# The last MLP units and the first units of the next projection taken by token tile, and the S5 products on tiles of the TensorE array

## The reference

```python
# end of the first block
h = rmsnorm(x, norm_mlp_g[l])
x = x + jnp.square(jax.nn.relu(h @ w_up[l])) @ w_down[l]      # 2048 -> 8192 -> 2048
return rmsnorm(x, norm_final_g)
...
# start of the second block
h = _rms(x, norm_g[l, 0]) * (1.0 + scale_m) + shift_m
proj = (h @ w_in[l]).astype(f32)                               # da_q, da_k, da_v, ..., s5_u
...
# S5 branch: 32 groups of 16 channels with 64 states each
bu = jnp.einsum('sgc,gpc->sgp', us, bb)                        # real and imaginary part
... (associative scan over tokens) ...
y = jnp.einsum('sgp,gcp->sgc', xr, c_re) - jnp.einsum('sgp,gcp->sgc', xi, c_im) + d_skip * us
```

## Time and profile before

| | |
|---|---|
| median of 3 runs | 2720.89 us (2720.29, 2720.89, and one of 9454.43) |
| the profiled execution | 2721.06 us, its span 2719.3 us |
| PE busy | 2650.8 us, 97% |
| DVE, ACT, POOL busy | 1906.8, 1254.7, 281.9 us |
| granted TensorE clock, mean | 0.992 |

### The profile page before, as it was taken

How to read it: one execution, slowest core, us unless ns; L and a number is a source line. 1 busy time by engine, 2 the same in 40 slices (tenths; PEclk the granted TensorE clock), 3 DMA queues, 4 the chain that set the end, 5 groups by cost and what they waited for, 6 DMA issues and landing times.

```text
span 2719.3 us, 36265 instructions
## 1 busy us (share of the span) xinstructions
PE 2650.8 (97%) x13230; PEld 2237.7 (82%) x13230; DVE 1906.8 (70%) x2275; ACT 1254.7 (46%) x1519; POOL 281.9 (10%) x322
## 2 busy tenths in 40 slices
PE   8999999999999998999999999999999999999997
PEld 8998888888888887898977788777778888888886
DVE  6777677788778777665686778687755555555687
ACT  5445544444444445455555444444554444444443
POOL 0040041324132000071000000000000000000000
PEclk9999999999999998999999999999999999999999
DMA  9646687788778885756554655588656656666784
GB/s 343 215 163 214 219 278 257 266 276 273 263 264 276 270 271 165 228 171 208 164 169 151 223 200 174 189 300 284 217 178 193 188 191 192 187 191 191 257 291 165
DMA packets 294705, 606.18 MB, mean 223 GB/s; under 512 B 25873, under 2 KB 26065, under 8 KB 292673
## 3 DMA queue, kind: packets, MB, share of 16 engines
q1 hardware_dynamic: 290272, 578.55, 64.8%
q0 software_dynamic: 4320, 26.13, 2.6%
HBM read 593.31 MB, written 11.29 MB: 222 GB/s over the span
## 4 chain that ended last, share of the span: by engine, by line
PE 86%; DVE 6%; ACT 3%; DMA 2%; issue 2%; POOL 0%; SPq 0%; DVEq 0%; ACTq 0%; POOLq 0%
PE ps L540 84%; DVE w_lo L1780 2%; ACT w_hi L1178 1%; DMA w_raw<-in_w_in 1%; DVE arena L1775 1%; PE ps L645 1%; DMA w_raw<-in_w_up 1%; DMA w_raw<-in_w_gate 0%; ACT arena L1209 0%; DVE x L1790 0%; PE ps L672 0%; PE ps L635 0%; DMA arena<-gain_scratch 0%; PE ps L656 0%; DVE arena L2375 0%
## 5 line engine op out<-in xcount | busy, mean ns | idle before, releaser
L1780 DVE TENSOR_TENSOR w_lo<-w_raw,w_hi 128x1024 fp32r<-128x1024 f32 x904 | 1127.0, 1250 | 765.0 <-ACT w_hi L1178 757.2
L1178 ACT ACTIVATE w_hi<-w_raw 128x1024 fp32r<-128x1024 f32 x904 | 951.1, 1054 | 1375.8 <-PE ps L540 1283.0
L540 PE MATMUL ps<-w_hi,hop_hi_part 128*128 128x512 f32 x2144 | 846.7, 395 | 8.1 <-issue 2.5
L540 PE MATMUL ps<-w_hi,hop_lo_part 128*128 128x512 f32 x2144 | 836.9, 390 | 0.0
L540 PE MATMUL ps<-w_lo,hop_hi_part 128*128 128x512 f32 x2144 | 836.8, 390 | 0.0
L540 PEld LDWEIGHTS ps<-w_hi,hop_hi_part 128*128 128x128 f32 x2144 | 403.9, 188 | 100.8 <-issue 13.4
L540 PEld LDWEIGHTS ps<-w_hi,hop_lo_part 128*128 128x128 f32 x2144 | 403.7, 188 | 85.1
L540 PEld LDWEIGHTS ps<-w_lo,hop_hi_part 128*128 128x128 f32 x2144 | 404.1, 188 | 81.6
L540 PE MATMUL ps<-w_hi,hid_hi_part 128*128 128x512 f32 x992 | 389.1, 392 | 2.8 <-DVE hid_lo_part L2447 1.5
L540 PE MATMUL ps<-w_hi,hid_lo_part 128*128 128x512 f32 x992 | 386.3, 389 | 0.0
L540 PE MATMUL ps<-w_lo,hid_hi_part 128*128 128x512 f32 x992 | 386.0, 389 | 0.0
(11 more groups left out here) (302 smaller groups left out, 1462.8 us busy)
## 6 DMA issues: line engine op xcount, KB each, us to landing
arena<-in_ada_w SPq DMA_DIRECT2D x256, 384.0 KB, 4.7
w_raw<-in_ffn_w_in SPq DMA_DIRECT2D x176, 512.0 KB, 3.5
w_raw<-in_w_in SPq DMA_DIRECT2D x152, 512.0 KB, 3.6
w_raw<-in_w_up SPq DMA_DIRECT2D x128, 512.0 KB, 3.9
w_raw<-in_w_down SPq DMA_DIRECT2D x128, 512.0 KB, 4.7
w_raw<-in_w_gate SPq DMA_DIRECT2D x128, 512.0 KB, 4.0
w_raw<-in_ffn_w_out SPq DMA_DIRECT2D x88, 512.0 KB, 3.6
w_raw<-in_w_out SPq DMA_DIRECT2D x64, 512.0 KB, 5.1
```

Of the source, the lines that this page charges most:

```text
L540: return nc.tensor.matmul(o, w, r, start=start, stop=stop, skip_group_check=True)
L1178: return nc.scalar.activation(o, i, ACT.Copy, scale=scale)
L1780: V.tensor_tensor(w_lo[:, j % LEAD, :, 0:cols], w_raw[:, j % RAW, :, 0:cols], w_hi[:, j % LEAD, :, 0:cols].bitcast(F32), ALU.subtract).the ...
```

## The change

1. The last four MLP units (20 to 23) run for token tile 0 first (four `token_half`), then for tile 1. DVE and ACT add, multiply and square the two parts per tile (`last_part`, `half_square`), and the variance and inverse root are made per tile.
2. The transposes of tile 0 (`turn_half(5, 0, ...)`) stand in front of the last `token_half` of the MLP. The first four projection units run for tile 0, then for tile 1, in the way of the FFN seam (`staggered_chunk`, shared by both now). For this the first chunk is da_v with `token_unit`, and the third is da_k with `unit`.
3. The ada slices of the last stretch stand at loop steps 0 to 15 (before 0 to 18), and PE's `modulation` after unit 17 (before 21).
4. `s5_input` takes the upper or lower 64 rows alone, in the order 0, 2, 1, 3; `s5_product` holds 32 columns and writes 32 partitions of bank 6.

```diff
-ADA_TAIL = [k + k // 4 for k in range(KT)]
+ADA_TAIL = list(range(KT))
...
         def last_group(u):
-            if u == 21:
+            if u == 17:
                 modulation((G_MLP + MLP_SUPER // 2) * KT)
-        down(R, 16, H + 3, 0, 1, MLP_SUPER, between=last_group)
...
+        for n in range(2):
+            token_chunk(R, 16 + UB * n, H + 3, n, hid_hi[:, 1], hid_lo[:, 1], UB, between=last_group)
+        for n in range(2):
+            pe.wait_ge(drained[n], H + 5)
         pe.wait_ge(sem["mod_ready"], G_IN2)
-        turn_scaled(5, 0)
+        for t in range(TT):
+            for q in range(STAGGER):
+                n, k = 2 + q // UB, q % UB
+                if t == 0:
+                    pe.wait_ge(sem["lo_ready"], R * 8 + (20 + q + 1))
+                elif q == 3:
+                    turn_half(5, 0, SCALED_TOK)
+                m = token_half(20 + q, n % 2, t, hid_hi[:, 1], hid_lo[:, 1], UK * k, k == 0, k == UB - 1)
+                if t == 1:
+                    m.then_inc(sem["unit_done"], 1)
+                elif k == UB - 1:
+                    m.then_inc(sem["half_done"], 1)
...
+        staggered_chunk(5, R_IN2, H_IN2, SCALED_TOK)
+        for c in range(1, 4):
+            chunk(R_IN2, UA * c, H_IN2 + c // 2, c % 2, ftiles=1 if c == 3 else FT, between=gain_steps)
...
-            for ii in range(4):
-                m = mm(PS[4 + ii // 2][:, (ii % 2) * S:(ii % 2 + 1) * S], span(S5_B[t % 2] + 2 * part, ii * P, P),
-                       T(40 + t), start=ii % 2 == 0)
+            for ii in (0, 2, 1, 3):
+                rows = slice(64 * (ii // 2), 64 * (ii // 2) + 64)
+                m = mm(PS[4 + ii // 2][:, (ii % 2) * S:(ii % 2 + 1) * S], span(S5_B[t % 2] + 2 * part, ii * P, P)[rows],
+                       T(40 + t)[rows], start=ii % 2 == 0)
...
-                m = mm(PS[6][:, 0:S], span(S5_C[t % 2] + 2 * part, ii * P, P), ROT[part][:, ii],
-                       start=part == 0 and ii == 0, stop=part == 1 and ii == 3)
+                own = 2 * S5_CH * ii
+                m = mm(PS[6][own:own + 2 * S5_CH, 0:S], span(S5_C[t % 2] + 2 * part, ii * P + own, 2 * S5_CH), ROT[part][:, ii],
+                       start=part == 0, stop=part == 1)
```

On ACT, behind the MLP loop (`both_squares(0)` stands at its step 18):

```diff
+        both_squares(1)
+        half_square(2, 0, 4)
+        half_square(3, 0, 8).then_inc(sem["tok_sums"], 1)
+        pair_guess(3, 0)
+        split(R_IN2, 0)
+        half_square(2, 1, 24)
+        split(R_IN2, 1)
+        hi_half(5, 0, 0)
+        hi_half(5, 0, 1)
+        half_square(3, 1, 28).then_inc(sem["tok_sums"], 1)
+        hi_half(5, 0, 2)
+        hi_half(5, 0, 3)
+        pair_guess(4, 1)
+        split(R_IN2, 2)
+        split(R_IN2, 3)
```

On DVE, behind the MLP loop (the modulation stands at its step 18, the addition of part 1 at step 19):

```diff
+        last_part(2, 0)
+        last_part(3, 0)
+        pair_variance(3, 0)
+        last_part(2, 1)
+        pair_inverse(3, 0)
+        mid_scaled(0, half(0)).then_inc(sem["rows_ready"], 1)
+        split(R_IN2, 0)
+        for b in range(2):
+            turned_half(5, 0, b, gain5, 0)
+        lo_half(5, 0, 0)
+        last_part(3, 1)
+        split(R_IN2, 1)
+        lo_half(5, 0, 1)
+        for b in range(2, STAGGER):
+            turned_half(5, 0, b, gain5, 0)
+        pair_variance(4, 1)
+        lo_half(5, 0, 2)
+        lo_half(5, 0, 3)
+        split(R_IN2, 2)
+        pair_inverse(4, 1)
+        mid_scaled(1, half(0)).then_inc(sem["rows_ready"], 1)
+        split(R_IN2, 3)
```

More of the change, by code:

```diff
@@ L848, in gain_steps @@
                 pe.wait_ge(sem["gain_ready"], 1)
-                pe.wait_ge(sem["xT_ready"], TURNED[5] + 4)
+                pe.wait_ge(sem["xT_ready"], TURNED[5] + 10)
                 turn_gain(4)
[L852 to L857, removed]
+        staggered_chunk(5, R_IN2, H_IN2, SCALED_TOK)
+        for c in range(1, 4):
+            chunk(R_IN2, UA * c, H_IN2 + c // 2, c % 2, ftiles=1 if c == 3 else FT, between=gain_steps)
         modulation((G_IN2 + 1) * KT, 6)
@@ L1449, in _ @@
                 projection_unit(c, q)
[L1451 to L1452 removed]
+                if c == 0 and q == 0:
+                    rest_rows(5, 3, gain5, 0)
                 if (c, q) == (1, 6):
@@ L1834, in lo_pair @@
                             ALU.subtract).then_inc(sem["hop_ready"], 2)
-        def scale_rows(dst, src, i):
-            for c in range(4):
-                for t in range(TT):
-                    m = V.tensor_scalar(dst[:, t, part(c)], src[:, t, part(c)], inverse(i, t), None, ALU.mult)
-                m.then_inc(sem["rows_ready"], 1)
         def of_arena(t):
@@ L2134, in _, with last_part @@
-        then(V.tensor_scalar(mid, mid, 1.0 / D, EPS, ALU.mult, ALU.add))
-        stt(both, mid, EPS, both, ALU.mult, ALU.add).then_inc(sem["tok_var"], 1)
-        token_inverse(3, SUM_MID, 2)
-        scale_rows(SCALED_TOK, Y_TOK, SUM_Y)
-        for b in range(4):
-            lo_pair(5, b)
+                    m = gained(t, n)
+                m.then_inc(sem["mid_gained"], 1)
+        def last_part(n, t):
+            k = 2 * t + n - 2
+            if t == 0:
+                dve.wait_ge(sem["half_done"], n - 1)
+            else:
+                dve.wait_ge(sem["unit_done"], (R_MLP + 29) * 8 + 20 + UB * (n - 1))
+            V.tensor_tensor(x_tok[:, t, part(n)], SETS[n % 2][t][:], x_tok[:, t, part(n)], ALU.add).then_inc(sem["mid_added"], 1)
+            dve.wait_ge(sem["mid_added"], k + 1)
+            gained(t, n).then_inc(sem["mid_gained"], 1)
+            if t == 1:
+                dve.sem_inc(drained[n % 2], 1)
@@ new lines, in pair_variance @@
+        def pair_variance(k, t):
+            mid, both = (tok_var[:, TT * i + t:TT * i + t + 1] for i in (SUM_MID, SUM_Y))
+            dve.wait_ge(sem["tok_sums"], k)
+            V.reduce_sum(mid, sums[:, SUM_MID, t], axis=AX_X)
+            then(V.reduce_sum(both, sums[:, SUM_Y, t], axis=AX_X))
+            V.tensor_scalar(both, both, 1.0 / D, None, ALU.mult)
+            then(V.tensor_scalar(mid, mid, 1.0 / D, EPS, ALU.mult, ALU.add))
+            stt(both, mid, EPS, both, ALU.mult, ALU.add).then_inc(sem["tok_var"], 1)
@@ new lines, in pair_inverse, with mid_scaled @@
+        def pair_inverse(k, t):
+            cols = slice(TT * SUM_MID + t, TT * SUM_Y + t + 1, TT)
+            dve.wait_ge(sem["tok_guess"], k)
+            then(newton(tok_inv[:, cols], tok_var[:, cols], tok_guess[:, cols]))
+        def mid_scaled(t, cols):
+            return V.tensor_scalar(SCALED_TOK[:, t, cols], Y_TOK[:, t, cols], inverse(SUM_Y, t), None, ALU.mult)
+        last_part(2, 0)
[3 more added lines that the diff above has]
+        pair_inverse(3, 0)
@@ L2142, in projection_unit @@
+        split(R_IN2, 3)
+        mid_scaled(0, part(2))
+        mid_scaled(1, part(2)).then_inc(sem["rows_ready"], 1)
+        turned_half(5, 1, 0, gain5, 0)
+        turned_half(5, 1, 1, gain5, 0)
+        for b in range(STAGGER):
+            lo_half(5, 1, b)
+            if b < 2:
+                turned_half(5, 1, b + 2, gain5, 0)
+        mid_scaled(0, part(3))
+        mid_scaled(1, part(3)).then_inc(sem["rows_ready"], 1)
         def projection_unit(c, q):
```

255 lines of the change are left out of this document (122 added, 133 removed).

## The result

| | before | changed |
|---|---|---|
| median | 2722.67 us (5 runs) | 2705.86 us (5 runs) |
| runs | 2720.29 to 2723.72 and the one of 9454.43 | 2704.38 to 2709.75 |
| the profiled execution, its span | 2721.06 us, 2719.3 us | 2709.75 us, 2708.0 us |

The ratio of the times is 0.9943, with a 95% interval of 0.9929 to 0.9956: 15.5 us less (12 to 19), clear of no change though far under 2%. The forecast was 2709 us, 12 us less, in a range of 2703 to 2719. The one run of 9454.43 us is not explained; the ratio leaves it out.

The account below looks back on a forecast made before the run. PE was taken as the bound, busy 2650.8 of 2719.3 us. S5 11.0 us (3.4 + 7.0 + 0.6) and the seam 1.0 make 12 us off the profiled 2721.06: 2709 us, range 2703 to 2719.

Parts of the forecast that it names:

- The seam gives more: Rival on the passage from MLP to projection: no falls of the clock, quicker DVE, 5 us gained, 2705 us; 13%.
- All four side by side: S5 products: the four 32-column matmuls run together, 0.86 us a group, 0.87 less, 7.0 us for eight groups.
- half side by side: Rival on S5 products: matmuls start only in order, 1.5 us a group, 0.23 less, time 2714 us; 17%.
- one behind the other: Rival on S5 products: the four column tiles run serially, 2.15 us a group, time 2719 us; 10%.
- every tile pays: Slower rival on S5 products: each column tile pays for getting in and out, 3.4 us a group, 2730 us; 4%.
- the price of getting in and out: S5 groups on small tiles: a cost on top of streaming, 0.41 to 0.43 us, read from groups on 64-row halves.
- S5 inputs: Input groups on 64-row halves: 1.31 us instead of 1.73, 0.42 less each, 3.4 us for eight.
- What standing together and starting from an idle PE add: S5: three adjacent product and input groups pay once, five products start from idle; up to 1.6 us, 0.6 taken.
- The waits for L2405 stay: S5 products: PE's four waits for DVE, 5.4 us, remain because PE's units start DVE's steps there.
- ACT splits it only behind the guess: First projection chunk: reason given for 3.0 us idle at unit 2, the guess needing tile 1's variance.
- restarts 0.6: Seam: the term for PE restarts, 0.6 us, within 56.2 us of work, restarts and idle time.
- The clock in the seam: Two falls to 0.50 cost 2.4 us, leaving 1.0 us gain; over 7 us at 0.5 would show the prediction wrong.

Follow-up runs that it names:

- e4: The changed kernel with all four S5 products of a group on one column tile (the S5 output is then wrong): 2717.19 us.
- e1: The changed kernel with both S5 steps as before, so the new seam alone: 2720.86 us, ratio 0.9987 to the kernel before.
- e2: The kernel before with only the two S5 steps put on tiles, seam as before: 2708.47 us, ratio 0.9946 to the kernel before.
- e8: The changed kernel with ACT instead of DVE moving the third and fourth part of the turned tile 0 out of PSUM: 2703.99 us.
- e11: The changed kernel run again as it is: 2706.16 us, ratio 0.9932 to the kernel before.
- e7: The changed kernel with PE waiting for each accumulation set separately and ACT moving two turned parts of tile 0 for DVE: 2704.88 us.
- e6: The changed kernel with ACT rounding projection unit 2 earlier, ahead of the third part of the activations and the guess for tile 1: 2703.08 us.
- e3: The changed kernel with the S5 inputs issued in the order 0, 1, 2, 3 instead of 0, 2, 1, 3: 2706.67 us.
- e5: The changed kernel with PE waiting for each accumulation set separately, and for the modulation only ahead of tile 0's transposes: 2703.11 us.

## Why the prediction was right, and where it was off

The forecast of 2709 us was 3 us too high, and its sign, its order of causes (S5 far ahead of the seam) and the idle times' places were right. The median of 2705.86 us lies beside the 2705 of "The seam gives more", but that rival is not what happened: of the missing 3 us the traces show 1.8 in the S5 groups, and the rest can't be put down to one place. The interval of 0.9929 to 0.9956 also shows that a change well under the 54 us that the prediction named can be told from none.

- **S5 products on four column tiles.** "All four side by side" held (group cost, starts within 0.02 us, and e4), and with it fell the three rivals on them: half side by side (1.5 us a group), one behind the other (2.15) and every tile pays (3.4). A group measured 0.77 us for 0.86. The mis-sized term is the price of getting in and out: 0.765 - 0.432 = 0.33 us here, not the 0.43 of the 64-row halves; for the 64-row inputs it is 0.40. Eight times 0.97 us are 7.7 for 7.0.
- **S5 inputs.** 1.27 us for 1.31: 0.46 less each, 3.7 us for 3.4.
- **What standing together and starting from an idle PE add.** I took 0.6; the traces give 12.8 - 7.7 - 3.7 = 1.4 us. About 0.9 of it come from the five products behind a wait: alone, a full group costs 1.97 us there for 1.73, a tiled one 0.84 for 0.77. The rest is the three places where both stand together: 1.90 us, where a product behind a wait and an input group would make 0.84 + 1.27 = 2.11. So "pay once for getting in and out" was too much: 0.2 us are saved, not the whole price.
- **The rest of the S5 stretch.** A further 2.4 us in this pair of traces were not in the sum: 0.7 us of wait and 1.7 us of low clock at the first product. They are not the change's: e1 and e2 show the wait and the fall going either way, by when the gate weights land. Without them the stretch gives 12.8 us, and the forecast's 11.0 is short by 1.8.
- **"The waits for L2405 stay."** Right: 4.7 us for 5.4, in four.
- **The seam.** Idle times forecast 0.5, 2.4, 1.9, 0.5, 1.4, 3.0, 1.0, 0.1, 1.2, 0.7, 0.6; measured 0.43, 2.13, 1.46, 0.35, 1.17, 2.57, 0.41, none, 1.35, 0.48, 0.27. Each stands where it was put; the sum is 10.6 for 13.3. Of the 1.9 for 1.46 us a part is a slip of the sum: the terms written down for tile 0 end at 13.55, not 13.8. For the 2.57 us the reason given ("ACT splits it only behind the guess") holds for 0.63 us; e8 shows DVE's row as the larger part.
- **The work in the seam.** The piece that the prediction puts at 56.2 us at full clock took 55.9 us in e11, which had no fall there. But idle time was 10.7 us of it, so work and restarts were 45.2 us for 42.9. The mis-sized term is "restarts 0.6": it should have been 2.9. In part this is how the rows count, since an idle time begins at a matmul's modelled end, 0.39 us behind its start, and a matmul costs only a step of 0.227; ten idle times hide 1.6 us so. The two errors cancel, and that the length came out right is luck.
- **The clock in the seam.** Two falls of 3.4 us for 2.4 us was right for the profiled run: 107.70 against 105.1 us without a fall, 2.6 us, so the seam gives 1.1 us in the pair of profiles for 1.0 forecast. It was not right for the kernel: of six traces with the changed seam two had no fall, one a single fall of 6.8 us, and two had 10.2 us at 0.50, which cost 4.2 us and is beyond the 7 us that the prediction named as a sign of being wrong. Over all traces the stretch takes 107.4 against 108.0 us, with a spread of 4 us, so "about 1 us" is the best that can be said; in a run without a fall it is 2.9.
- **The end of the program.** The sum had no term for it. The kernels with the new seam take 2 us more there on average, which is of the size of what the seam gives; that the seam is the cause is not shown beyond the split into two and eleven traces.
- **The run itself.** The sum was made on one profiled execution. The start to unit 17 differs by up to 5.6 us between runs of nearly the same code, which is as large as most terms of this prediction. That the profiled time met the forecast to 0.8 us is luck: 3.6 us more at the start and 2.9 at the end stand against 4.3 more in the S5 stretch and 1.5 between seam and S5, none of which was in the sum.

Still open: what decides whether the clock falls behind the same idle time, why the start varies, and why the write near the end lands later with the new seam.

## To carry to other kernels

Where a product has blocks of zeros, split it along them and put the pieces on different tiles of the array, but count some 0.3 to 0.4 us for getting in and out of the small shape. Here groups of four fp32 matmuls of 256 columns gained 0.46 us on two row halves and 0.97 us on four column tiles (smaller groups were not tried), and two groups of different shapes next to each other saved 0.2 us of that price. When a long wait is cut into short ones, ask of each wait whether all it names is needed at that point (PE waited for both sets and the modulation, and needed one set) and whether work that waits for nothing stands right behind it (the S5 inputs): these two questions, and one step moved from the full engine to the less busy one, gave 3.6 us in the edited stretches (7.2 by the medians), where the whole reordering of the seam gave 1.3 by the medians and 1 to 6 by the interval. Judge edits of 1 or 2 us by the length of the stretch in the trace, not by medians, and look at the stretches that you did not edit too: the loss at the end of this program shows only there.

## What was not expected of the hardware

- Four matmuls on 32-column tiles cost 0.33 us above their streaming time of two steps of 0.216, less than four on two 64-row tiles (0.40). On one column tile they cost 2.05 us, more than as full blocks (1.73).
- The same idle times of 2.13 and 2.57 us in the same program were followed by 3.4 to 6.8 us at the 1.2 GHz level in some runs and by none in others (3 of 8, 4 of 7), and this moves a stretch of 105 us by up to 4.2 us.
- Idle times of 1.16 to 2.04 us ahead of the first S5 product were followed by no fall in ten traces; those of 2.19 and 2.77 us were, in both. The length alone does not decide: at the end of the program 2.30, 2.44 and 2.46 us had no fall (e7, e8, e6) and 2.09 and 2.10 us had one (e3, e5).
- A write of 8 KB near the end landed in 1.6 to 1.7 us in two kernels and in 2.3 to 2.7 us in the eleven with the new seam, which lies 1600 us earlier.
